# A two-block transformer kernel: 1/rms of the second block's norms applied behind the matmuls instead of to the rows

## The chip, the cores and the metric

One core of one Trainium2 chip. The metric is the device time of one execution in microseconds, median of several runs. Engines: TensorE (PE; its weight loads are PEld), VectorE (DVE), ScalarE (ACT), GpSimd (POOL), and SyncE (SP), which here only issues DMAs. Each engine runs its own instructions in order; semaphores order the engines against each other.

## What is computed

The input is 256 tokens of width 1024. A first block (three kinds of attention or recurrence, an output projection, a mixture of 16 experts) is followed by the second block, two layers of

```
h = h + 0.5 * swiglu(rmsnorm(h, g[0]), ...)      # feed-forward, 2816 wide
u = rmsnorm(h, g[1])
h = h + mixer(u)                                 # layer 0: hybrid attention, layer 1: sliding window
h = h + 0.5 * swiglu(rmsnorm(h, g[2]), ...)
...
def rmsnorm(x, g):
    return x * rsqrt(mean(x * x, -1) + EPS) * g
def swiglu(x, w1, w3, w2):
    return (silu(x @ w1) * (x @ w3)) @ w2
```

and a last rmsnorm. The factor rsqrt(...) is one number per token, so it can be applied to x, or to anything that is linear in x.

## The kernel before

**State.** x_res holds the 256 tokens as T = 2 blocks of 128 rows (tokens on partitions) by 1024 columns. All weights are streamed from HBM as "slots" of 128 x 3072 floats (1.5 MB), each in three pieces a, b, d of 512 KB. SP loads a piece into raw once the piece two slots earlier has been split. Matmuls run on rounded operands (fp32r), and every operand is split into a rounded part and its remainder: ACT writes w_hi (L546), DVE writes w_lo = raw - w_hi (L937). A product is three matmuls: hi by hi, hi by lo, lo by hi (L1537 to L1539; in feed-forward tiles L1718 to L1721 with hi and lo of x side by side, 512 columns).

**Feed-forward** (`feed_forward`, one version per engine): 22 tiles, one slot each. PE forms gate and up of 128 hidden columns (banks 4 to 7 of PSUM, alternating by tile), 16 steps over the 8 column blocks k of x; DVE sums the two halves of a bank (L1083), ACT takes silu (L670), DVE multiplies and splits h (L1107 to L1110); PE adds the down product of the tile before (banks 0 to 3). Behind the last tile DVE adds half of banks 0 to 3 into x_res (L1118), block 0 behind `y_tile`, block 1 behind `d_used`. The experts (`experts_by_group`) end in a scatter product and the same additions (L1177).

**Projections** (`proj`): a slot is three weight tiles of 128 columns. Results with tokens on partitions ("N", "W") are made for both blocks; those turned ("T") for all 256 tokens at once. ACT copies them out of PSUM (L569), or DVE adds them to x_res (L957). The hybrid layer has 8 slots, the sliding one 4, each output projection 3.

**A norm** (c = 0 to 11; 4, 5, 7, 8, 9, 11 belong to the second block's hidden state, 6 and 10 only turn the attention's output). In order: ACT squares both blocks with a running sum (L606, `ssq_ready`); POOL adds epsilon and takes the power -0.5 (L460, L462, `rstd_ready`); DVE scales block 0 (L970, `xs_ready`), ACT block 1 (L616, `xs1_ready`) into `scaled`; PE turns 16 squares of 128 x 128 into PSUM (L1543, `tr_ready` for each two column blocks); ACT rounds them times the gain into xT_hi (L628, `xt_hi`); DVE forms the remainder xT_lo (L982, `xt_lo`). PE starts the next stage as soon as the first two column blocks are there. While it waits it runs filler matmuls (`keep_busy`, L1550), 14 of them for one norm.

**Attention** works on units of one head pair and one token block: DVE adds the bias to the scores times a constant (L1003), and so on. The order of work on every engine is written out by hand.

Of the kernel before, what the change touches and what calls it, by code (L numbers as in the profile page):

```python
# [99 lines left out]
def block_program(nc, wstream, x_in, mem_in, pos_in, pos_cols_in, pcol_in, prow_in, smallw_in, const_in, table_in, bias_lookup_in,  # L100
                  bias_dram, out):
    ctx = ExitStack()
    with ctx:
# [24 lines left out]
        stat = sb("stat", [P, 256])  # L128
# [36 lines left out]
        def stats(n):  # L165
            o = taken[0]
            taken[0] += n
            assert taken[0] <= 256
            return stat[:, o:o + n]
# [18 lines left out]
        mqgain = stats(1)  # L188
        mixgain = stats(8)
# [77 lines left out]
        zb = at(16, 16, 2 * P)  # L267

# [27 lines left out]
        flat += [("T", v[:, j, :]) for v in (h_qaT, h_kaT, h_kbT) for j in range(4)]  # L296
# [3 lines left out]
        flat = [("T", s_qT[:, j, :]) for j in range(8)] + [("T", s_kT[:, j, :]) for j in range(2)] + [("N", s_v, 0)]  # L300
# [6 lines left out]
        def psum_places(n):  # L307
# [3 lines left out]
            n_first = [j for j, it in enumerate(tiles) if it[0] != "T"]  # L311
# [3 lines left out]
            for j, it in enumerate(tiles):  # L315
                if it[0] != "T":
# [52 lines left out]
        def g_of(i):  # L369
# [5 lines left out]
            dict(src=x_res, gain=g_of(0), norm=True), dict(src=x_res, gain=g_of(1), norm=True),  # L375
            dict(src=mixed, gain=onegain, norm=False), dict(src=x_res, gain=g_of(2), norm=True),
            dict(src=x_res, gain=g_of(3), norm=True), dict(src=x_res, gain=g_of(4), norm=True),
            dict(src=mixed, gain=onegain, norm=False), dict(src=x_res, gain=g_of(5), norm=True)]
# [4 lines left out]
        normed = [sum(n["norm"] for n in norms[:c]) for c in range(len(norms))]  # L383

        def turned(c, k):

            bank = k // 2 if c == 1 else 4 + k // 2
            return ps[:, bank, S * (k % 2):S * (k % 2) + S]

# [63 lines left out]
        def _(pool):  # L453
            def inverse_rms(i):

                pool.wait_ge(S_("ssq_ready"), i + 1)
                if i:
                    pool.wait_ge(S_("xs_ready"), i)
                    pool.wait_ge(S_("xs1_ready"), i)
                nc.gpsimd.tensor_scalar(meansq, ssq, RMS_EPS, None, ALU.add).then_inc(S_("meansq_ready"), 1)  # L460
                pool.wait_ge(S_("meansq_ready"), i + 1)
                nc.gpsimd.tensor_tensor(rstd, meansq, minus_half, ALU.pow).then_inc(S_("rstd_ready"), 1)  # L462

# [44 lines left out]
            pool.wait_ge(S_("y_added"), 2)  # L508
# [21 lines left out]
        def _(act):  # L530
# [24 lines left out]
            def evacuate_slot(n):  # L555

                act.wait_ge(S_("d_used"), n + 1)
                pair, n_first, places = psum_places(n)
                last = None
                groups = []  # L560
                for j, it, views in places:
                    if it[0] == "T":
                        groups.append((it[1], views[0]))
                    elif it[0] == "W":
                        groups += [(it[1][:, t, :], views[t][:, 0:8]) for t in range(T)]
                    else:
                        groups += [(it[1][:, t, it[2]:it[2] + P], views[t]) for t in range(T)]
                for dst, src in groups:
                    last = nc.scalar.activation(dst, src, ACT.Copy)  # L569
                last.then_inc(S_("evacuated"), 1)  # L570

# [15 lines left out]
            def norm(c, wait=None):  # L587
                norm_squares(c, wait)
# [3 lines left out]
            def norm_squares(c, wait=None):  # L592
                n = norms[c]
                if n["norm"]:
                    if c:
                        act.wait_ge(S_("xs_ready"), normed[c])
                    for t in range(T):

                        if c:
                            if wait[0] == "evacuated" and not t:  # L600
                                act.wait_ge(S_("half_added"), RESIDUAL_ENDS.index(wait[2]) + 1)
                            else:
                                act.wait_ge(S_(wait[0]), wait[1] + t if wait[0] == "y_added" else wait[1])
# [4 lines left out]
                    ins.then_inc(S_("ssq_ready"), 1)  # L608
# [12 lines left out]
            def norm_turned(c):  # L621
                n = norms[c]
                for q in range(4):
                    if c == 0 and q == 2:
                        split_hi(0, "d")
                    act.wait_ge(S_("tr_ready"), 4 * c + q + 1)
                    for k in (2 * q, 2 * q + 1):
# [1592 lines left out]
```

## Time and profile before

| | us |
|---|---|
| median of 3 runs (1635.41 to 1640.03) | 1635.64 |
| span of the profiled execution | 1634.7 |
| PE busy | 1552.5 (95%) |
| DVE busy | 1140.4 (70%) |
| ACT busy | 814.9 (50%) |
| mean granted TensorE clock | 0.984 of full speed |

The page says for each engine how much of the span it worked; the timeline gives single instructions with their start and length, and in brackets how long the engine had been idle before and who released it; windows give the same sums for chosen stretches. A busy PE may be running fillers. Times of the trace count from the first instruction.

### The profile page before, as it was taken

The page shows a single profiled execution, that of the slowest core. Times are in us where ns is not written, and L with a number is a line of the kernel's source. Part 1 is how long each engine was busy: PE and PEld are TensorE (multiplying, and loading weights), DVE is VectorE, ACT ScalarE, POOL GpSimd, SP SyncE. Part 2 cuts the span into 40 slices and gives each one's busy share as a digit, 9 for nine tenths or more (in the row PEclk, how much of TensorE's full clock was granted, in tenths as well). Part 3 has the DMA queues.
Part 4 walks back from the last instruction along what each step waited for, and adds up shares of the span by engine and source line. Part 5 has one row for each costly group of instructions (what it writes and reads, how often), then busy time and mean ns, then how long its engine had stood idle before and what let it go on. Part 6 is the DMA issues. An engine that isn't in the chain of part 4 may idle for free.

```text
span 1634.7 us, 27257 instructions
## 1 busy us (share of the span) xinstructions
PE 1552.5 (95%) x9282; PEld 1350.7 (83%) x9282; DVE 1140.4 (70%) x1741; ACT 814.9 (50%) x1309; POOL 45.2 (3%) x53
## 2 busy tenths in 40 slices
PE   7998798999999989999999999999999999999997
PEld 6887686888898958888898788888788878888886
DVE  5845864888798847777646567777777764677775
ACT  6423553777677744334544554443533355554442
POOL 1120000000000000000000200000000000000000
PEclk9999999999999999999999899999999999999999
DMA  7312231999799947555442355556455544255652
GB/s 260 116 62 81 78 113 37 323 348 344 257 345 344 354 169 225 190 185 187 137 155 78 106 185 188 191 192 193 155 187 184 188 136 154 78 166 186 189 191 77
DMA packets 82151, 299.70 MB, mean 183 GB/s; under 512 B 9279, under 2 KB 9407, under 8 KB 81953
## 3 DMA queue, kind: packets, MB, share of 16 engines
q1 hardware_dynamic: 79632, 289.97, 52.8%
q0 software_dynamic: 2160, 8.66, 1.7%
q8 instruction: 47, 0.77, 0.2%
q14 instruction: 24, 0.19, 0.0%
q10 hardware_dynamic: 288, 0.12, 0.0%
HBM read 297.59 MB, written 1.11 MB: 183 GB/s over the span
## 4 chain that ended last, share of the span: by engine, by line
PE 84%; DVE 9%; ACT 4%; issue 2%; POOL 1%; DMA 0%; DVEq 0%; SPq 0%; POOLq 0%; ACTq 0%
PE ps L1721 18%; PE ps L1537 15%; PE ps L1538 14%; PE ps L1539 14%; PE ps L1719 10%; PE ps L1718 3%; PE ps L1543 2%; DVE w_lo L937 2%; PE ps L1671 1%; PE ps L1814 1%; DVE xT L982 1%; PE ps L1738 1%; ACT w_hi L546 1%; PE ps L1643 1%; DVE stat L1005 1%
## 5 line engine op out<-in xcount | busy, mean ns | idle before, releaser
L937 DVE TENSOR_TENSOR w_lo<-raw,w_hi 128x1024 fp32r<-128x1024 f32 x549 | 653.6, 1221 | 216.3 <-ACT w_hi L546 214.8
L546 ACT ACTIVATE w_hi<-raw 128x1024 fp32r<-128x1024 f32 x549 | 549.2, 1055 | 339.8 <-PE ps L1539 307.3
L1721 PE MATMUL ps<-xT,w_hi 128*128 128x512 f32 x1232 | 439.6, 396 | 0.0
L1719 PE MATMUL ps<-xT,w_lo 128*128 128x256 f32 x1408 | 364.5, 279 | 0.0
L1719 PEld LDWEIGHTS ps<-xT,w_lo 128*128 128x128 f32 x1408 | 265.3, 188 | 16.1
L1721 PEld LDWEIGHTS ps<-xT,w_hi 128*128 128x128 f32 x1232 | 231.2, 188 | 47.1
L1537 PE MATMUL ps<-w_hi,xT 128*128 128x256 f32 (+2 forms) x848 | 261.6, 308 | 7.1 <-DVE w_lo L937 3.6
L1538 PE MATMUL ps<-w_lo,xT 128*128 128x256 f32 (+2 forms) x848 | 251.0, 296 | 0.0
L1539 PE MATMUL ps<-w_hi,xT 128*128 128x256 f32 (+2 forms) x848 | 250.7, 296 | 0.0
L1537 PE MATMUL ps<-w_hi,h_hi 128*128 128x512 f32 x480 | 188.4, 393 | 4.4 <-DVE h_lo L1143 4.4
L1538 PE MATMUL ps<-w_lo,h_hi 128*128 128x512 f32 x480 | 188.1, 392 | 0.0
L1539 PE MATMUL ps<-w_hi,h_lo 128*128 128x512 f32 x480 | 187.4, 391 | 0.0
L1537 PEld LDWEIGHTS ps<-w_hi,xT 128*128 128x128 f32 x848 | 160.8, 190 | 24.5 <-issue 21.3
L1538 PEld LDWEIGHTS ps<-w_lo,xT 128*128 128x128 f32 x848 | 161.3, 190 | 0.1
L1539 PEld LDWEIGHTS ps<-w_hi,xT 128*128 128x128 f32 x848 | 161.0, 190 | 0.0
L1083 DVE TENSOR_REDUCE arena<-ps 128x256 f32<-128x512 f32 x176 | 121.1, 688 | 38.2 <-PE ps L1721 38.2
L1543 PE MATMUL ps<-const,arena 128*128 128x128 f32 x416 | 76.7, 306 | 34.3 <-ACT arena L616 18.7
L1539 PEld LDWEIGHTS ps<-w_hi,h_lo 128*128 128x128 f32 x480 | 90.5, 189 | 19.7
L1537 PEld LDWEIGHTS ps<-w_hi,h_hi 128*128 128x128 f32 x480 | 90.5, 189 | 18.3 <-DVE h_lo L1143 4.7
L1538 PEld LDWEIGHTS ps<-w_lo,h_hi 128*128 128x128 f32 x480 | 90.5, 189 | 16.9
L1543 PEld LDWEIGHTS ps<-const,arena 128*128 128x128 f32 x416 | 53.8, 156 | 50.5 <-issue 20.2
L670 ACT ACTIVATE arena<-arena 128x256 f32<-128x256 f32 x88 | 36.8, 418 | 113.4 <-DVE arena L1083 113.4
(319 smaller groups left out, 1648.4 us busy)
## 6 DMA issues: line engine op xcount, KB each, us to landing
raw<-in_wstream SPq DMA_DIRECT2D x549, 512.0 KB, 4.9
arena<-bias_rows POOLq DMA_DIRECT2D x2, 2048.0 KB, 12.6
const<-in_const POOLq DMA_DIRECT2D x1, 1112.0 KB, 7.7
x_res<-in_x SPq DMA_DIRECT2D x2, 512.0 KB, 4.4
arena<-in_mem POOLq DMA_DIRECT2D x1, 1024.0 KB, 6.4
out<-arena SPq DMA_DIRECT2D x2, 512.0 KB, 2.7
smallw<-in_smallw POOLq DMA_DIRECT2D x1, 768.0 KB, 4.5
prow<-in_prow POOLq DMA_DIRECT2D x1, 512.0 KB, 5.2
```

The lines of the kernel that those rows point to most:

```text
L546: nc.scalar.activation(w_hi[:, slot, lo:hi], raw[:, slot, lo:hi], ACT.Copy).then_inc(S_(f"hi_{part_}"), 1)
L670: nc.scalar.activation(silu[:, f % 2, :], gate_sum[:, f % 2, :], ACT.Silu).then_inc(S_("silu_ready"), 1)
L937: tt(w_lo[:, slot, lo:hi], raw[:, slot, lo:hi], w_hi[:, slot, lo:hi].bitcast(F32), ALU.subtract).then_inc(S_(f"lo_{part_}"), 1)
L982: ins = stt(xT_lo[:, k, :], turned(c, k), n["gain"][:, k:k + 1], xT_hi[:, k, :].bitcast(F32), ALU.mult, ALU.subtract)
L1083: return nc.vector.tensor_reduce(dst[:, b, :], ps[:, bank, :].rearrange("p (a s) -> p s a", a=2), AX.X, ALU.add)
L1537: a = mm(out_, stat_[0], mov[0], start=start, stop=False)
L1538: b = mm(out_, stat_[0], mov[1], start=False, stop=False)
L1539: c = mm(out_, stat_[1], mov[0], start=False, stop=stop)
L1543: return nc.tensor.transpose(out_, in_, ident)
L1718: mm(bank, w_hi[:, s, c:c + P], both, start=True, stop=False)
L1719: low = mm(bank[:, 0:S], w_lo[:, s, c:c + P], xT_hi[:, k, :], start=False, stop=False)
L1721: last = mm(bank, w_hi[:, s, c:c + P], both, start=False, stop=k == KD - 1)
```

## The change

In norms 4, 5, 7, 8, 9 and 11 nothing is scaled in front of the turns any more: x_res itself is turned, rounded and split. 1/rms is applied later:
- feed-forward: DVE multiplies the gate sum by a row that holds 1/rms of each token (`rstd_row`), in every one of the 4 x 22 tiles; the up sum stays unscaled, and the final addition multiplies by 0.5/rms per token (`rstd_part`).
- projections: values and the other "N" results are scaled as ACT copies them (`scale=rstd`); keys (new kind "K", 9 hybrid tiles, 2 sliding ones) are written by DVE times `rstd_row` (`k_out`); queries stay unscaled, and the scores of kinds a and c are multiplied by 1/(8 rms) of the query token.
- `rstd_row` comes from two matmuls of PE (`rstd_rows`: 1/rms broadcast against the identity) and a copy by ACT (`rstd_row_out`). In a feed-forward they stand in the second tile, in a projection behind the first slot.

With it: the square of block 1 moves behind the rounding and the next slot's splits; turns stand in banks 0 to 3, 6 and 7, in groups (0), (1), (2), (3), (4, 5), (6, 7); behind an output projection the turns of column blocks 0 to 5 are done inside its last slot; the fillers go; piece d of the next slot is split by DVE behind the norm; the first tile or slot takes its steps by column block, gate and up together. `y_added` counts halves. The core of the diff:

```diff
@@ VectorE: norm, keys @@
-            def norm(c):
-                norm_scale(c)
-                norm_lo(c)
+            def norm(c, slot=None, after=None):
+                if not late[c]:
+                    norm_scale(c)
+                norm_lo(c, slot, after)
+
+            def k_out(n):
+                dve.wait_ge(S_("row_ready"), lates[5 if n < HOUT0 else 9] + 1)
+                dve.wait_ge(S_("d_used"), n + 1)
+                if all_k(n):
+                    dve.wait_ge(S_("evacuated"), evac_until(n - 1))
+                for dst, src in k_tiles(n):
+                    ins = tt(dst, src, rstd_row, ALU.mult)
+                ins.then_inc(S_("evacuated" if all_k(n) else "k_scaled"), 1)
...
@@ VectorE: end of norm_lo @@
+                if after == len(groups[c]):
+                    split_lo(slot, "d")
...
@@ ScalarE: norm @@
             def norm(c, wait=None):
+                if late[c]:
+                    norm_squares(c, wait, (0,))
+                    if c not in AFTER_FF:
+                        act.wait_ge(S_("d_used"), wait[2])
+                    norm_turned(c)
+                    return
...
@@ ScalarE: feed_forward tile, behind split_hi of a and b @@
+                    if c is not None and f == 0:
+                        norm_squares(c, wait, (1,))
+                        rstd_row_out(c)
...
@@ ScalarE: evacuate_slot @@
+                if n in k_slots:
+                    act.wait_ge(S_("k_scaled"), k_slots.index(n) + 1)
...
@@ VectorE: feed_forward tile @@
-                    summed(gate_sum, 4 + 2 * b).then_inc(S_("gate_summed" if f0 else "moe_gate_summed"), 1)
+                    def gate_scaled():
+                        dve.wait_ge(S_("gate_raw"), plus(at_f + f + 1, i, per))
+                        tt(gate_sum[:, b, :], gate_sum[:, b, :], rstd_row, ALU.mult).then_inc(S_("gate_summed"), 1)
+
+                    summed(gate_sum, 4 + 2 * b).then_inc(S_("moe_gate_summed" if gated else "gate_raw"), 1)
+                    if f and not gated:
+                        gate_scaled()
                     if n + 1 < N_SLOTS:
                         split_lo(n + 1, "b", i, per)
                     dve.wait_ge(S_("b_used"), plus(n + 1, i, per))
                     summed(up_sum, 5 + 2 * b).then_inc(S_("up_summed" if f0 else "moe_up_summed"), 1)
+                    if not f and not gated:
+                        dve.wait_ge(S_("row_ready"), lates[c] + 1)
+                        gate_scaled()
...
-                    if n + 1 < N_SLOTS:
+                    if f < tiles - 1:
                         split_lo(n + 1, "d", i, per)
...
-                        ins = stt(x_res[:, t, 512 * half:512 * half + 512], ps[:, 2 * t + half, :],
-                                  1.0 if gated else 0.5, x_res[:, t, 512 * half:512 * half + 512], ALU.mult, ALU.add)
-                    ins.then_inc(S_("y_added"), 1)
+                        stt(x_res[:, t, 512 * half:512 * half + 512], ps[:, 2 * t + half, :],
+                            1.0 if gated else rstd_part[:, t:t + 1], x_res[:, t, 512 * half:512 * half + 512], ALU.mult,
+                            ALU.add).then_inc(S_("y_added"), 1)
...
@@ TensorE @@
+            def late_norm(c):
+                y = 4 * AFTER_FF[c]
+                pe.wait_ge(S_("y_added"), y + 2)
+                for k in (0, 1, 4, 5, 6, 7):
+                    turn(c, k, 0)
+                pe.wait_ge(S_("y_added"), y + 3)
+                turn_last(c, 0)
+                turn_last(c, 1)
+                turn_both(c, 2)
+                pe.wait_ge(S_("y_added"), y + 4)
+                turn_both(c, 3)
+                turn_last(c, 4, 5)
+                turn_last(c, 6, 7)
+
+            def late_norm_open(c, n):
+                pe.wait_ge(S_("evacuated"), evac_until(n - 1))
+                for k in range(4):
+                    turn_both(c, k)
+                turn_both(c, 4, 5)
+
+            def late_norm_close(c, n):
+                pe.wait_ge(S_("half_added"), RESIDUAL_ENDS.index(n + 1) + 1)
+                turn(c, 6, 0)
+                turn(c, 7, 0)
+                pe.wait_ge(S_("evacuated"), evac_until(n))
+                turn_last(c, 6, 7)
+
+            def rstd_rows(c):
+                pe.wait_ge(S_("rstd_ready"), normed[c] + 1)
+                for t in range(T):
+                    ins = mm(ps[:, 0, P * t:P * t + P], rstd[:, t:t + 1].broadcast_to([P, P]), ident, start=True, stop=True)
+                ins.then_inc(S_("row_psum"), 1)
...
@@ TensorE: feed_forward tile @@
+                        if f == 1 and not g and k == KD // 2 and call is not None:
+                            rstd_rows(call)
...
@@ TensorE: down product @@
+                    if not f and call is not None:
+                        pe.wait_ge(S_("row_ready"), lates[call] + 1)
...
-            norm(7, added=("evacuated", evac_until(FFB0 - 1)))
+            late_norm_close(7, FFB0 - 1)
             feed_forward(*ffs[2], 7)
-            norm(8, added=("y_added", 6))
+            late_norm(8)
```

## Rows read from the trace of the kernel before

**Rows 1.** The page, part 1: busy us of the engines, share, instructions.

```profile
PE 1552.5 (95%) x9282; PEld 1350.7 (83%) x9282; DVE 1140.4 (70%) x1741; ACT 814.9 (50%) x1309; POOL 45.2 (3%) x53
```

**Rows 2.** Windows at six norms: length; busy PE, PEld, DVE, ACT, POOL; clock; DMA; GB/s.

```profile
604.63:612.69 8.06, 6.54 (x33) 4.13 (x31) 3.06 (x6) 4.20 (x9) 2.48 (x3) 1.00 0.19 65
795.84:804.22 8.38, 6.12 (x31) 3.96 (x30) 3.96 (x8) 5.33 (x11) 0.94 (x2) 1.00 0.00 0
953.70:960.52 6.82, 5.74 (x33) 4.06 (x31) 2.20 (x5) 4.66 (x11) 0.94 (x2) 1.00 0.41 147
1143.66:1152.02 8.36, 6.12 (x31) 3.97 (x30) 3.96 (x8) 5.33 (x11) 0.93 (x2) 1.00 0.01 4
1335.16:1343.52 8.36, 6.12 (x32) 3.97 (x30) 3.97 (x8) 5.33 (x11) 0.93 (x2) 1.00 0.01 4
1435.16:1441.96 6.80, 5.73 (x33) 4.05 (x31) 2.20 (x5) 4.66 (x11) 0.93 (x2) 1.00 0.39 145
```

**Rows 3.** Timeline at norm 8: start, us, engine, line, operation, tiles, [idle before <-releaser].

```profile
1142.07 0.39 PE L1539 MATMUL ps<-w_hi,h_lo 128*128 128x512 f32 x1
1142.23 1.23 DVE L937 TENSOR_TENSOR w_lo<-raw,w_hi 128x1024 fp32r<-128x1024 f32 x1 [1.87 <-ACT w_hi L546]
...
1143.38 2.48 DVE L1118 SCALAR_TENSOR_TENSOR x_res<-ps,x_res 128x512 f32<-128x512 f32 x4
...
1143.43 0.39 PE L1539 MATMUL ps<-w_hi,h_lo 128*128 128x512 f32 x1
...
1144.75 1.06 ACT L606 ACTIVATE arena<-x_res 128x1024 f32<-128x1024 f32 x1 [2.55 <-DVE x_res L1118]
...
1145.90 3.26 PE L1550 MATMUL ps<-xT 128*128 128x512 f32 x10 [1.18 <-DVE x_res L1118]
...
1147.42 0.71 POOL L462 TENSOR_TENSOR stat<-stat 128x2 f32<-128x2 f32 x1
...
1149.46 1.94 PE L1543 MATMUL ps<-const,arena 128*128 128x128 f32 x16 [0.30 <-ACT arena L616]
1150.12 3.03 ACT L628 ACTIVATE xT<-ps,pcol 128x256 fp32r<-128x256 f32 x8 [0.81 <-PE ps L1543]
1151.00 3.23 DVE L982 SCALAR_TENSOR_TENSOR xT<-ps,pcol,xT 128x256 fp32r<-128x256 f32 x8 [2.08 <-ACT xT L628]
...
1152.02 0.47 PE L1718 MATMUL ps<-xT,w_hi 128*128 128x512 f32 x1 [0.62 <-DVE xT L982]
...
1155.08 0.40 PE L1718 MATMUL ps<-xT,w_hi 128*128 128x512 f32 x1
```

**Rows 4.** Timeline at norm 7: the last matmul of the projection and the addition behind it.

```profile
953.58 0.28 PE L1539 MATMUL ps<-w_hi,xT 128*128 128x256 f32 x1
...
953.90 0.42 DVE L957 TENSOR_TENSOR x_res<-ps,x_res 128x256 f32<-128x256 f32 x1 [0.99 <-PE ps L1539]
```

**Rows 5.** Timeline at norm 4: the additions of block 1 behind the experts.

```profile
605.23 1.29 DVE L1177 TENSOR_TENSOR x_res<-ps,x_res 128x512 f32<-128x512 f32 x2 [5.58 <-PE ps L1814]
```

**Rows 6.** Twenty steady tiles of a feed-forward (windows), and a 256-wide DVE multiply (groups).

```profile
1160.30:1324.50 164.20, 164.20 (x870) 140.70 (x869) 119.00 (x160) 64.72 (x78) 0.00 (x0) 1.00 0.60 192
...
L1107 DVE TENSOR_TENSOR h_hi<-arena 128x256 fp32r<-128x256 f32 x88 | 37.5, 426 | 15.7 <-DVE arena L1083 15.1
```

**Rows 7.** Hybrid projections: timeline of ACT, of DVE, then the window behind them.

```profile
864.15 1.06 ACT L569 ACTIVATE arena<-ps 128x256 f32<-128x256 f32 x5 [4.36 <-PE ps L1539]
...
872.48 1.13 ACT L569 ACTIVATE arena<-ps 128x128 f32<-128x128 f32 x6 [3.40 <-PE ps L1539]
...
867.39 3.50 DVE L937 TENSOR_TENSOR w_lo<-raw,w_hi 128x1024 fp32r<-128x1024 f32 x3
...
871.00:883.00 12.00, 12.00 (x69) 11.20 (x67) 0.00 (x0) 6.25 (x16) 0.00 (x0) 1.00 0.36 116
```

**Rows 8.** Windows in front of norm 10: no matmul issued, then the clock.

```profile
1408.00:1409.00 1.00, 0.00 (x1) 0.00 (x0) 0.89 (x4) 0.00 (x0) 0.00 (x0) 1.00 0.00 0
1409.50:1412.50 3.00, 3.00 (x16) 3.00 (x16) 1.24 (x3) 2.09 (x6) 0.00 (x0) 0.50 0.00 0
```

More of the change, by code:

```diff
@@ L310, in psum_places @@
             tiles = projections[n]
-            n_first = [j for j, it in enumerate(tiles) if it[0] != "T"]
+            n_first = [j for j, it in enumerate(tiles) if it[0] not in "TK"]
             at_n = len(n_first) * P
@@ L383, in block_program, with k_tiles, all_k @@
         normed = [sum(n["norm"] for n in norms[:c]) for c in range(len(norms))]
+        late = ["late" in n for n in norms]
+        lates = [sum(late[:c]) for c in range(len(norms))]
+        early_scaled = [sum(n["norm"] and "late" not in n for n in norms[:c]) for c in range(len(norms) + 1)]
+        groups = [((0,), (1,), (2,), (3,), (4, 5), (6, 7)) if late[c] else ((0, 1), (2, 3), (4, 5), (6, 7))
+                  for c in range(len(norms))]
+        group_base = [sum(len(g) for g in groups[:c]) for c in range(len(norms))]
+        LATE_BANK = (0, 1, 2, 3, 6, 6, 7, 7)
+        AFTER_OUT = {FFB0: 7, FFD0: 11}
+        AFTER_FF = {4: 0, 5: 1, 8: 2, 9: 3}
         def turned(c, k):
+            if late[c]:
+                col = S * (k % 2) if k >= 4 else 0
+                return ps[:, LATE_BANK[k], col:col + S]
             bank = k // 2 if c == 1 else 4 + k // 2
             return ps[:, bank, S * (k % 2):S * (k % 2) + S]
+        def k_tiles(n):
+            pair, n_first, places = psum_places(n)
+            return [(it[1], views[0]) for j, it, views in places if it[0] == "K"]
+        def all_k(n):
+            return n in projections and len(k_tiles(n)) == len(projections[n])
+        k_slots = [n for n in projections if n in range(HYB0, HOUT0) or n in range(SWA0, SOUT0)]
+        k_slots = [n for n in sorted(k_slots) if k_tiles(n) and not all_k(n)]
         ffs = [(MOE0, MOE_TILES, 0), (FFA0, FF_TILES, MOE_TILES), (FFB0, FF_TILES, MOE_TILES + FF_TILES),
@@ L659, in attention, with feed_forward @@
                         exp_unit(i)
-            def feed_forward(n0, tiles, f0):
+            def feed_forward(n0, tiles, f0, c=None, wait=None):
                 def tile(f, i=None, per=0):
@@ L1576, in transposed @@
             def transposed(c, k):
-                if c is not None and k % 2 == 0:
-                    pe.wait_ge(S_("xt_lo"), 4 * c + k // 2 + 1)
+                if c is not None:
+                    for g, ks in enumerate(groups[c]):
+                        if ks[0] == k:
+                            pe.wait_ge(S_("xt_lo"), group_base[c] + g + 1)
             def proj(n, c=None):
@@ L1706, in tile @@
                         pe.wait_ge(S_("h_ready"), plus(f0 + f - 1, i, per))
-                    for g in range(2):
-                        if not g or not by_k:
-                            for part_ in "ab" if by_k else "ab"[g]:
+                    both_first = by_k or not f
+                    steps = [(g, k) for g in range(2) for k in range(KD)]
+                    if not f:
+                        steps.sort(key=lambda s: s[1])
+                    for g, k in steps:
+                        if not k and not (g and both_first):
+                            for part_ in "ab" if both_first else "ab"[g]:
                                 pe.wait_ge(S_(f"hi_{part_}"), plus(n + 1, i, per))
@@ L2014, in _ @@
                 feed_forward(*ffs[0], None)
-            norm(4, added=("y_added", 2))
+            late_norm(4)
             feed_forward(*ffs[1], 4)
-            norm(5, added=("y_added", 4))
+            late_norm(5)
             proj(HYB0, 5)
+            rstd_rows(5)
             proj(HYB0 + 1)
@@ L2066, in _ @@
                 proj(n, 10 if n == SOUT0 else None)
-            norm(11, added=("evacuated", evac_until(FFD0 - 1)))
+            late_norm_close(11, FFD0 - 1)
             feed_forward(*ffs[4], 11)
```

227 lines of the change are left out of this document (143 added, 84 removed).

## Prediction

> **What bounds the kernel now.** I read the page's engine line first: TensorE (PE) is busy 95% of the span, VectorE (DVE) 70%, ScalarE (ACT) 50% [rows 1]. So time can come only out of places where PE has no useful matmul to run. Next I cut the trace at the six norms that the change touches (norms 4, 5, 7, 8, 9, 11; 7 and 11 stand behind an output projection, the others behind an expert or feed-forward stage). Each window of [rows 2] runs from the issue of the first thing behind the last useful matmul to the issue of the first matmul of the next stage: 8.06, 8.38, 6.82, 8.36, 8.36 and 6.80 us, 46.8 us in all. PE looks busy in them (5.7 to 6.5 us), but that is filler matmuls and the 16 turns. The timeline of norm 8 [rows 3] shows what the window is made of, one thing behind the other: DVE still splits the last piece of the next slot (1142.23 to 1143.46) though the first half of PE's sums was there earlier; four additions into x_res; two Squares on ACT; the pow on POOL, ended 1148.13; the scaling of the rows; 16 turns from 1149.46; ACT's rounding from 1150.12; DVE's remainder from 1151.00; first matmul 1152.02. Everything between the additions and the turns is there only for 1/rms.
>
> **The change, part by part.** All sums are against the profiled execution, whose span is 1634.7 us; the median of the runs is 1635.64, 0.9 above it, and I keep that distance.
>
> *Norm behind a feed-forward (norms 5, 8, 9; clock times are norm 8's).* DVE's split of piece d moves behind the norm, so the additions of block 0 wait only for PE's matmul of 1142.07, which ends 1142.46. An addition starts 0.04 behind the end of its matmul (953.58 + 0.28, then 953.90) [rows 4], so 1142.50. From the first addition to the first Square it took 1144.75 - 1143.38 = 1.37 [rows 3], so Square of block 0 runs 1143.87 to about 1145.0. The matmul of 1143.43 ends 1143.82, so block 1 is added from 1143.86, one half in 0.62 (2.48 / 4). Its first half releases the turn of column block 0 at 1144.5; from turn to ACT took 0.66 for four turns, for one about 0.4, so ACT is ready for it at 1145.0, just as Square ends. One rounding 0.43, one remainder 0.44 and 0.14 to PE (the steps of [rows 3], halved because the first group now holds one column block, not two): first matmul at 1146.1, a gap of 2.44. Saved: 8.38 - 2.44 = 5.94, and 5.92 twice.
>
> *Norm behind the experts (norm 4).* Block 0's Square is over long before; block 1's additions start at 605.23 [rows 5]. 0.65 for one half, 0.4, 0.43, 0.44, 0.14 give 607.35 against 612.69: 5.34 saved.
>
> *Norm behind a projection (norms 7, 11).* Twelve turns move into the last slot's matmuls: they now lengthen it, at (1.94 - 0.27) / 15 = 0.11 each by 1.33. After the last matmul (953.58 + 0.28 for norm 7) [rows 4] ACT's rounding can start at once, it waits for the slot's end only because it overwrites xT; DVE's addition (0.42) runs beside it. 0.04 + 0.43 + 0.45 + 0.14 behind the end: gap 1.25 counted from the window's start. Saved 6.82 - 1.33 - 1.25 = 4.24, and 4.22.
>
> Together 31.6 us.
>
> *The first tile.* It now takes gate and up by column block, 5.5 / 8 = 0.69 of matmuls each against 0.40 for one remainder (3.23 / 8), so nothing starves; before, the first half tile took 1155.08 - 1152.02 = 3.06 [rows 3], where the pace of the steady tiles is (8.21 - 12 x 0.227) / 2 = 2.75 (8.21 from [rows 6], 0.227 from the six matmuls between 1142.07 and 1143.43). That gives back 0.3 at four norms and 0.15 at the two in front of a projection: +1.5. The two matmuls that spread 1/rms into a row are new on PE: no row shows this form; between 0.11 (a turn at full clock) and twice that (at half), I take 0.12 each plus their semaphore, 0.25 per norm: -1.5. At norm 9 the moved split of piece d follows the remainders (ends about 1341.5) and PE wants it at about 1341.2: -0.3.
>
> *What moves off the chain but stays work.* The Square of block 1 now stands on ACT behind the rounding and two splits of the next slot. For norm 8: rounding 1145.0 to 1147.9, splits until 1150.0; first Square's start to pow's end was 3.38 with two Squares, so 2.3 with one: 1/rms at 1152.3. PE asks for it in the middle of the second tile's gate, 1146.1 + 5.5 + 1.4 = 1153.0. Slack 0.7, so cost zero; the cover is the first tile. Queued behind this wait on PE is the rest of that tile; ACT waits too (row copy, then silu). DVE sums the first gate until 1152.5, splits a piece until 1153.6, sums up until 1154.3, multiplies by the row (there at 1154.1) until 1154.7; silu, three short DVE operations: h at about 1156.4. The first down product asks for it at 1146.1 + 2 x 5.5 + 0.25 = 1157.4. If the chain were late, each us late costs a us, up to about 2 per norm.
>
> *The added multiply of the gate sum.* 88 tiles, each one DVE multiply of 128x256: 0.43 [rows 6]. In the steady state DVE works 119.0 of 164.2 us (20 tiles) and PE 164.2 of 164.2 [rows 6], so 5.95 of 8.21 per tile becomes 6.4. Free while that holds. The chain gate sum, multiply, silu, h is longer by 0.45, and h is wanted a tile later (in the last tile behind the 2.7 us of the down product before it). Constants in the final addition and the scores become per-partition columns; the remainder, which reads such a column, takes 0.40 per 256 elements, no more than the plain multiply, so zero.
>
> *Keys.* Nine key tiles of the hybrid stage and two of the sliding one are now written by DVE (0.43 each, about 3.9 us) instead of ACT. DVE has nothing at all from 871 to 883 while PE is full [rows 7], which hides it. The tight place is slot 5 of the hybrid stage: ACT emptied it at 864.15, now it waits for DVE's multiply, which stands behind the index scores, where DVE's splits of slot 7 began (867.39, later by one multiply of three tiles less what ACT's lighter queue brings forward): about 868.2. The splits of slot 7 slip with it by 3 to 4 us, the first piece to about 871.4, wanted at 872.4, where slot 6 ends (ACT empties it at 872.48). Slack 1.0; the load behind it lands later too. I put 0.1 there and 0.2 on the last sliding slot, where ACT waits for one DVE multiply in front of the attention: -0.3. Bounds 0 and 3.
>
> Sum: 31.6 + 1.5 - 1.5 - 0.3 - 0.3 = **31.0 us**. Span 1603.7, median **1604.6**.
>
> *The fillers.* 14 wide filler matmuls per norm go. In the trace PE had nothing to run from 1408 to 1409, behind a run of short matmuls, and right behind that the granted clock was 0.50, 1.2 GHz, for three us [rows 8]. In the new gaps the idle stretches are shorter (turns stand between them, about 0.3 each; about 0.8 behind a projection) and dense matmuls stand in front of them; in the windows of [rows 2], with idle stretches of up to 1.18 (the filler of 1145.90) [rows 3], the clock stayed at 1.00, 2.4 GHz. So I count no loss.
>
> The Trainium skill, "TensorE: Matmul & The Clock Gate", section "What's actually happening", says that the throttled clock is the default and that activity releases it. That speaks against taking fillers out. The trace agrees that the clock can fall at a boundary; whether the new boundaries are quiet enough no row says. By the rule taken strictly the time would be the first rival's 1614.8.
>
> **The rivals.**
> *The clock falls at the six boundaries.* For: the stretch of [rows 8]. Against: less idle time than in today's windows. Three to four us of matmuls at half clock cost 1.5 to 2, I take 1.7: six of them 10.2, time 1614.8.
> *PE waits for 1/rms in the second tile.* For: slack of only 0.7, with ACT's loads and splits in front. Against: nothing on ACT there waits for data today. Late by 1.5 at each norm: 9 us, time 1613.6.
> *It does only half of what it says.* Another wait, the weights' splits or PSUM banks that turns and sums now share, ends last in the gaps: 2.5 us lost at each norm: 15, time 1619.6.
> *Slower: DVE becomes the bound of the steady tiles.* The gate multiply sits before silu in the loop. It decides once DVE needs over 8.21 us per tile. Each of 88 tiles would then be longer by up to 0.43, 38 us on top of 1604.6: 1642.4. Against: 1.8 us of room per tile.
>
> **How the numbers follow.** Forecast 0.74, clock 0.12, 1/rms 0.07, half 0.04, slower 0.03. The likeliest case alone spans 1600 to 1609 (bounds of keys, row matmuls, and the low-clock stretches in the attention, which may fall elsewhere when everything before them moves: one more or less is 1.7). For 8 in 10 the upper end reaches to the first two rivals: 1599 to 1615. 0.3% of this kernel is 4.9 us, about what can be told from no change. Faster 0.96, within 0.01, slower 0.03.
>
> **What the profile would show.** Gaps between the last useful matmul and the next of about 2.4 us (2.7 at norm 4; behind projections 1.25, with 12 turns inside the last slot). ACT's rounding starting as block 0's Square ends. No PE idle in front of the two row matmuls. Steady windows of 164.2 us for 20 tiles as before, with DVE at about 128. Clock 1.00 in the first tile behind each norm. It is wrong if a steady tile is longer than 8.21, if PE idles over 0.5 in the second tile, or if the hybrid stage up to its attention is longer than before by over 1 us.

## The result: 0.5% faster, 28 us slower than predicted

| | before | after |
|---|---|---|
| median | 1639.74 us (20 runs) | 1632.31 us (20 runs, 1617.62 to 1643.87) |
| span of the profiled execution | 1634.7 | 1640.6 |
| mean granted clock, profiled | 0.984 | 0.957 |

Time after / before is 0.9947, 95% interval 0.9925 to 0.9968; this ratio leaves out slow executions, those over 1.5% above the fastest of their kernel. 1604.6 was predicted, with 1599 to 1615 as the range. The forecast was counted down from 1635.64, the median of three runs; over 20 runs the kernel before takes 1639.74. So 4.1 of the 27.7 us by which the forecast missed lie in its starting point, and 23.6 in the change: 31.0 us were to be saved, the medians differ by 7.4. The spread of the changed kernel is wide, and it goes with the granted clock: its 20 executions have mean clocks from 0.956 (1641.6 us) to 0.976 (1617.6 us).

The page of after, its parts 1 and 2 (busy us; the clock in 40 slices of the span, tenths of full speed), answers [rows 1]:

```profile
PE 1570.0 (96%) x9222; PEld 1370.7 (84%) x9222; DVE 1175.8 (72%) x1834; ACT 808.9 (49%) x1298; POOL 50.5 (3%) x59
...
PEclk9998999999999999999998599999999997799999
```

The same line of before:

```profile
PEclk9999999999999999999999899999999999999999
```

PE executes fewer matmuls (9222 for 9282) but is busy 17.5 us longer. The two dips of after, slices 22 to 23 and 34 to 35, are the two attention stages of the second block.

The six gaps and the twelve early turns of norms 7 and 11 as windows (columns as in [rows 2]: length; busy PE, PEld, DVE, ACT, POOL; clock; DMA), then 20 steady tiles, which answer [rows 6]:

```profile
611.24:613.69 2.45, 2.29 (x17) 1.67 (x16) 1.92 (x4) 1.14 (x4) 0.00 (x0) 1.00 0.03 10
797.08:799.66 2.58, 2.35 (x17) 1.72 (x17) 2.26 (x5) 2.17 (x6) 0.00 (x0) 1.00 0.01 3
963.53:964.87 1.34, 0.82 (x6) 0.38 (x5) 1.05 (x3) 1.14 (x4) 0.00 (x0) 1.00 0.90 284
1148.28:1150.87 2.59, 2.35 (x18) 1.73 (x17) 2.26 (x5) 2.18 (x6) 0.00 (x0) 1.00 0.00 0
1334.32:1336.90 2.58, 2.34 (x17) 1.72 (x17) 2.26 (x5) 2.17 (x6) 0.00 (x0) 1.00 0.01 3
1446.20:1447.54 1.34, 0.82 (x7) 0.38 (x5) 1.06 (x3) 1.14 (x4) 0.00 (x0) 1.00 0.84 333
959.36:960.59 1.23, 1.23 (x15) 1.23 (x13) 1.23 (x2) 0.00 (x0) 0.00 (x0) 1.00 0.70 77
...
1161.00:1325.20 164.20, 164.20 (x871) 140.72 (x870) 127.44 (x182) 68.06 (x81) 0.00 (x0) 1.00 0.60 196
```

The gaps were to be 2.7 (norm 4), 2.44 (norms 5, 8, 9) and 1.25 behind 1.33 of early turns. They are 2.45, 2.58, and 1.34 behind 1.23, all at full clock. Against [rows 2] they save 5.61 + 5.80 + 4.25 + 5.77 + 5.78 + 4.23 = 31.4 us; 31.6 was forecast. What took it back is in the windows of after's attention stages, and two of before beside them:

```profile
890.00:934.00 44.00, 43.93 (x179) 33.84 (x179) 21.87 (x45) 18.46 (x66) 10.66 (x8) 0.50 0.11 36
1378.00:1415.00 37.00, 37.00 (x165) 30.34 (x165) 17.53 (x39) 18.65 (x70) 0.00 (x0) 0.50 0.00 1
```

```profile
894.00:904.00 10.00, 9.79 (x42) 7.24 (x40) 6.36 (x16) 4.86 (x19) 1.96 (x2) 0.50 0.01 2
1383.00:1408.00 25.00, 24.35 (x190) 19.71 (x189) 17.47 (x42) 19.79 (x76) 0.00 (x0) 1.00 0.01 2
```

After works most of its attention at 1.2 GHz: 165 matmuls of the sliding stage take 37 us where before 190 took 25. Cutting both traces at the same points gives the whole sum (positive: after is longer):

| part | us |
|---|---|
| before norm 4, code the change doesn't touch (37.5 us at 0.50 in after, 23.9 in before, 34.1 in a second trace of before) | +6.6 |
| six gaps | -31.4 |
| feed-forwards +0.24, +0.27, +0.31, +0.18, end +0.12 | +1.1 |
| hybrid projections up to the first scores (78.19 to 79.20) | +1.0 |
| hybrid output projection +0.73 (still at 0.50 where it starts), sliding one -0.06 | +0.7 |
| sliding projections up to the first scores (35.32 to 36.71) | +1.4 |
| hybrid attention, first scores to norm 6 (45.18 to 56.59) | +11.4 |
| sliding attention, first scores to norm 10 (30.45 to 46.23) | +15.8 |
| norm 10 (before 3.27, at low clock; after 2.59, at full) | -0.7 |
| sum, and the difference of the spans | +5.9 |

### The profile page after: what moved, and what is told of

The parts are those of the page before. It is cut to its first block, busy times and chain, and to the rows that moved or that the text cites. A ratio compares the mean times of both kernels' runs of the same rounds, so it can differ in the third digit from the quotient of the medians.

```text
span 1640.6 us, 27255 instructions
## 1 busy us (share of the span) xinstructions
PE 1570.0 (96%) x9222; PEld 1370.7 (84%) x9222; DVE 1175.8 (72%) x1834; ACT 808.9 (49%) x1298; POOL 50.5 (3%) x59
## 4 chain that ended last, share of the span: by engine, by line
PE 88%; DVE 8%; ACT 2%; issue 1%; DMA 0%; DVEq 0%; POOL 0%; SPq 0%; POOLq 0%; ACTq 0%
PE ps L1888 17%; PE ps L1634 15%; PE ps L1635 14%; PE ps L1636 14%; PE ps L1886 10%; PE ps L1640 3%; PE ps L1885 3%; PE ps L1831 2%; PE ps L1803 2%; DVE w_lo L1001 2%; PE ps L1981 1%; PE ps L1905 1%; DVE xT L1059 1%; ACT w_hi L580 1%; PE ps L2063 1%
## 5 line engine op out<-in xcount | busy, mean ns | idle before, releaser
L1640 PE MATMUL ps<-const,arena 128*128 128x128 f32 x320 | 71.9, 342 | 29.7 <-ACT arena L670 16.1
L1640 PEld LDWEIGHTS ps<-const,arena 128*128 128x128 f32 x320 | 47.0, 175 | 47.4 <-issue 25.7
```

The source lines that it names most:

```text
L1640: return nc.tensor.transpose(out_, in_, ident)
```

## The experiments

Three questions: is the low clock in the attention the change's doing or chance, what tips it, and what is the change worth without it? The table gives medians, mean clock of the profiled execution, the two attention stages in its trace (first scores to the turns of norm 6 and of norm 10), and the low-clock stretch that begins around the scores of the hybrid stage's sixth unit, where PE has waited for DVE to finish the fourth (the expectations call it the fourth unit). "None" means none there: several traces have a second stretch of 3.4 or 6.8 us at the end of the hybrid stage or behind it, e3 among them.

| kernel | median us | clock | hybrid | sliding | low stretch, sixth hybrid unit |
|---|---|---|---|---|---|
| before | 1638 to 1640 | 0.984 | 45.2 | 30.5 | 10.2 |
| c1 before again | 1638.3 | 0.983 | 44.2 | 30.5 | 10.2 |
| after | 1632.3 | 0.957 | 56.6 | 46.2 | 51.2 |
| c2 after again | 1633.4 | 0.963 | 48.5 | 48.3 | 23.9 |
| c3 after, fillers in sliding | 1627.9 | 0.981 | 48.3 | 35.3 | 23.9 |
| c4 before, same fillers | 1644.7 | 0.978 | 45.2 | 35.6 | 10.2 |
| d1 after, fillers only at its start | 1615.5 | 0.974 | 48.6 | 31.6 | 23.9 |
| d2 after, sliding keys as before | 1631.5 | 0.955 | 56.6 | 47.7 | 51.2 |
| d3 after, fillers in the gaps | 1634.0 | 0.970 | 48.6 | 46.3 | 23.9 |
| d4 c3 and two per hybrid unit | 1615.7 | 0.987 | 43.4 | 35.3 | none |
| e1 before, late sliding start | 1657.2 | 0.968 | 45.2 | 48.1 | 10.2 |
| e2 after, best fillers | 1608.8 | 0.990 | 43.4 | 31.6 | none |
| e3 before, same fillers | 1638.2 | 0.984 | 42.9 | 31.3 | none |
| e4 after, constant in hybrid scores | 1626.5 | 0.967 | 44.4 | 48.3 | 10.2 |
| f1 before, column in hybrid scores | 1640.2 | 0.988 | 44.6 | 30.4 | 10.2 |
| f2 e4 again | 1620.8 (2 runs) | 0.968 | 48.1 | 48.2 | 23.9 |

**Both kernels again (c1, c2).**

> The kernel before, unchanged, for its granted clock in many executions. In the profiled execution of the changed kernel, time lost to low clock has a price of its own: both attention stages of the second block ran at 0.50 nearly throughout (45.2 to 56.6 us and 30.5 to 46.2 us, first scores to the turns of norms 6 and 10). Theory A (the change moves these stages into the low clock): here the clock is 0.98 to 0.985 in most executions, and the two stages are near 45 and 30.5 us in the profile. Rival B (the low clock falls on the attention by chance in either kernel, and the profiled execution of before was a lucky one): clocks spread over 0.96 to 0.985, and a second profile shows one of the two stages over 10 us longer.

> The changed kernel, unchanged, for a second trace. Theory A: the two attention stages are again at 0.50 for most of their length (about 56 and 46 us), whatever the first block does. Rival B: at least one of them is at full clock (45 or 30 us) here. The gaps at the six norms stay at 2.5 us (1.3 behind the projections) in either case.

Before: ratio 0.9985 (0.9959 to 1.0011), all 12 executions at clock 0.974 to 0.988. After: 0.9897 (0.9811 to 0.9983). Of 86 executions of the kernel before with a recorded clock, 5 took 1655 us or more, at 0.960 to 0.970; of 24 of the changed kernel, 22 were at 0.972 or below. So the low clock comes with the change (theory A), though not with it alone: before falls into it now and then.

**Fillers in the sliding attention (c3, c4).**

```diff
-                if u < ATT4[0]:
-                    keep_busy(ps[:, 2 * (u % 2), :], 1)
+                keep_busy(ps[:, 2 * (u % 2), :], 1)
...
-                    if i == u0 + 1 and u0 == ATT2[0]:
+                    if i == u0 + 1 and u0 in (ATT2[0], ATT4[0]):
                         keep_busy(ps[:, 7 - u0 // QUAD % 2, :], 10)
...
+            keep_busy(ps[:, 0, :], 6)
             pe.wait_ge(S_("evacuated"), evac_until(SOUT0 - 1))
             attention(*ATT4)
```

> The changed kernel with filler matmuls in the sliding attention as the hybrid one has them: six in front of it, ten behind its second unit, one (0.21 us) ahead of each unit's scores. At full clock they cost at most 32 x 0.21 = 6.8 us less what PE waits there (about 4): up to 3 us. Theory A with few columns per us as what keeps the clock low: the sliding attention runs at full clock, 46.2 us become 31 to 34, time 1632.3 - 12 to 15 = about 1619. Rival C (the clock's fall comes from something other than the attention's own matmuls): the stage stays at 0.50 and gets longer by the fillers at half clock, 32 x 0.43 = up to 13 us, time 1635 to 1645.

> The kernel before with the same fillers in the sliding attention. Its stage ran at full clock in the profile (30.5 us), so fillers can't win there: theory A expects 0 to 3 us more than before (1636 to 1643). Rival B (before falls low there in many executions too): up to 5 us less in the median.

In the trace of c3 the sliding stage is at full clock, 35.3 us. Its median moved less than expected (1627.9, not 1619): four of nine executions took 1611.9 to 1620.5, at clocks from 0.977, the others 1627.9 to 1633.5 at 0.966 to 0.973, and of these there is no trace. In before the fillers lengthen the stage by 5.1 us in the trace (35.6 for 30.5), where 0 to 3 was expected; over all executions the ratio is 1.0025 (0.9996 to 1.0053), which leaves no cost just possible. One filler per unit lies on the path.

**Where the fall starts (d1, d2).** d1 keeps c3's last two edits and drops the first. d2 makes the two sliding keys kind "T" again, copied by ACT, and gives their scores a constant (the sliding keys and queries lack 1/rms).

```diff
-        flat = [("T", s_qT[:, j, :]) for j in range(8)] + [("K", s_kT[:, j, :]) for j in range(2)] + [("N", s_v, 0)]
+        flat = [("T", s_qT[:, j, :]) for j in range(8)] + [("T", s_kT[:, j, :]) for j in range(2)] + [("N", s_v, 0)]
```

> The changed kernel with fillers only where the sliding attention starts: six behind the projections, ten behind the second unit, none ahead of the other units. Theory A1 (what makes the clock fall is the quiet stretch at the stage's start, 1372.3 to 1377.9 in the changed kernel, where PE works 2.9 of 5.8 us; once low it stays low): the stage runs at full clock, about 31 us, the clock of the run is 0.975 or more, time about 1615 to 1620, and as good as with fillers ahead of each unit (1627.9 in the median, 1617.6 in the profiled execution). Rival A2 (the units' own matmuls have too few columns, fillers ahead of each are needed): the stage is at 0.50 for most of its length, time about 1632.

> The changed kernel with the sliding keys as before: ACT copies them unscaled, DVE multiplies nothing, and the scores get a constant instead of a column (so the sliding keys and queries lack 1/rms, and the scores are scaled down to stay in range). Theory A3 (the keys' way over DVE makes the quiet stretch at the start 0.5 us longer, and that tips the clock): PE waits 0.8 us for the first scores instead of 1.34, the stage is at full clock in most executions as in the kernel before, clock 0.97 to 0.98, time about 1618. Rival A4 (the delay is not what tips it): stage at 0.50 for 45 us, time about 1632.

d1: 1615.5 (4 runs, 1609.0 to 1619.7), ratio 0.9842 (0.9818 to 0.9866), sliding stage 31.6. Fillers at the start alone do it, with the units' own matmuls unchanged: A2 falls, and A1 fits. The start of the stage on PE in before, after and d1 (timelines: start, us, engine, line, tiles, [idle before]):

```profile
1378.84 0.93 PE L1643 MATMUL ps<-arena 64*128 64x128 f32 x8 [0.81 <-ACT arena L569]
1380.37 0.49 PE L1643 MATMUL ps<-arena 64*128 64x128 f32 x4 [0.61 <-DVE stat L1005]
1381.29 0.44 PE L1543 MATMUL ps<-const,arena 128*128 128x128 f32 x2 [0.42 <-ACT arena L637]
...
1383.31 0.56 PE L1671 MATMUL ps<-arena 128*128 128x64 f32 x4
```

```profile
1373.61 0.93 PE L1803 MATMUL ps<-arena 64*128 64x128 f32 x8 [1.34 <-issue]
1375.30 0.49 PE L1803 MATMUL ps<-arena 64*128 64x128 f32 x4 [0.76 <-DVE stat L1085]
1376.21 0.44 PE L1640 MATMUL ps<-const,arena 128*128 128x128 f32 x2 [0.42 <-ACT arena L691]
...
1378.71 0.95 PE L1831 MATMUL ps<-arena 128*128 128x64 f32 x4
```

```profile
1362.11 1.55 PE L1647 MATMUL ps<-xT 128*128 128x512 f32 x6
1363.59 0.93 PE L1803 MATMUL ps<-arena 64*128 64x128 f32 x8
1364.44 2.57 PE L1647 MATMUL ps<-xT 128*128 128x512 f32 x10
```

PE waits 0.81 + 0.61 + 0.42 in front of its first three groups in before, 1.34 + 0.76 + 0.42 in after: 0.68 longer. The last row of the first two shows the fall: the same four matmuls take 0.56 in before and 0.95 in after. Why it is longer stands on ACT and DVE (before in the first two views, after in the third):

```profile
1378.06 0.72 ACT L569 ACTIVATE arena<-ps 128x256 f32<-128x256 f32 x3 [4.46 <-PE ps L1539]
```

```profile
1379.44 0.42 DVE L1003 SCALAR_TENSOR_TENSOR arena<-ps,arena 128x256 f32<-128x256 f32 x1 [4.20 <-issue]
```

```profile
1372.88 0.63 ACT L611 ACTIVATE arena<-ps,stat 128x128 f32<-128x128 f32 x2 [4.73 <-PE ps L1636]
...
1372.37 0.42 DVE L1038 TENSOR_TENSOR arena<-ps,arena 128x256 f32<-128x256 f32 x1 [2.58 <-PE ps L1636]
1374.30 0.48 DVE L1083 SCALAR_TENSOR_TENSOR arena<-ps,stat,arena 128x256 f32<-128x256 f32 x1 [1.51 <-PE ps L1803]
```

DVE's key stands in front of ACT's two copies (0.5), and the score operation takes 0.48 instead of 0.42. d2 takes the key away, but the first two waits are still 1.04 and 0.71 where A3 had counted on 0.8 for the first, and the stage is still low in its trace (47.7), with executions at 0.955 and 0.960 beside ones at 0.971 and 0.980. A3 is not borne out as written: the key alone doesn't decide. No run brings the wait of the changed kernel back to 0.81.

**The gaps (d3).** Fillers around the turns of norms 4, 5, 8 and 9, with the identity as weights; behind an output projection (norms 7 and 11) there are only two, behind the last turns:

```diff
+            def keep_warm(n):
+                for _ in range(n):
+                    mm(ps[:, 4, 0:S], ident, const[:, 0:S], start=True, stop=True)
...
+                keep_warm(2)
                 pe.wait_ge(S_("y_added"), y + 2)
                 for k in (0, 1, 4, 5, 6, 7):
                     turn(c, k, 0)
+                keep_warm(1)
...
                 turn_last(c, 6, 7)
+                keep_warm(2)
```

> The changed kernel with filler matmuls back in the six gaps: two of 0.43 us (128 wide weights, 256 columns, full precision) in front of the turns, one in the middle, two behind them. They cost about 0.6 to 1 us per gap, 4 to 6 us in all. Rival B2 (the change pays for the fillers it took out: the chip's clock remembers the boundaries): the attention stages run at full clock more often, clock 0.97 or more, time 1620 to 1628. Theory A (the attention's clock is decided by what stands at the attention): nothing changes there, clock 0.955 to 0.97, time 1636 to 1639.

1634.0, sliding stage 46.3, hybrid 48.6. Both stages are still low with the gaps filled, and the time is outside B2's 1620 to 1628: B2 is not borne out. The clock of its ten executions, 0.963 to 0.973, is somewhat above after's, so a small effect isn't excluded.

**The delay put into before (e1).**

```diff
+                if n == SOUT0 - 1:
+                    groups[-1:-1] = [(scaled[:, 0, P * e:P * e + P], groups[-1][1]) for e in range(3)]
                 for dst, src in groups:
                     last = nc.scalar.activation(dst, src, ACT.Copy)
```

> The kernel before with one edit: in the last sliding projection slot ACT makes three idle copies of 128x128 (about 0.2 us each) ahead of its last one, so that PE waits about 1.4 us for the first scores instead of 0.81, as it does in the changed kernel (1.34). Nothing else differs: norms, fillers and scores are the old ones. Theory A1 (a quiet stretch at the start that is 0.6 us longer is enough to tip the clock for the whole stage): the sliding attention falls to 0.50 in most executions, 30.5 us become 46, clock about 0.965 instead of 0.982, median 1650 to 1656. Rival A6 (the tipping needs something else that the change brings): the stage stays at full clock as in the kernel before, median 1640, one execution in ten long.

All seven executions took 1652.6 to 1659.0; ratio 1.0104 (1.0073 to 1.0134). Its timeline and a window of the stage:

```profile
1381.16 0.93 PE L1645 MATMUL ps<-arena 64*128 64x128 f32 x8 [1.32 <-ACT arena L571]
1382.69 0.49 PE L1645 MATMUL ps<-arena 64*128 64x128 f32 x4 [0.61 <-DVE stat L1007]
```

```profile
1386.00:1424.00 38.00, 38.00 (x172) 31.34 (x171) 17.72 (x41) 19.07 (x72) 0.00 (x0) 0.50 0.00 1
```

Half a microsecond more of waiting (1.32 for 0.81) at the start of a 30 us stage costs 17.6 us (48.1 for 30.5), with none of the change in the kernel. That such a wait is enough is shown by this; that it is the whole of what tips the changed kernel is likely by d1 and e1, not shown.

**Hybrid stage (d4, e4, f1, f2).** d4 is c3 with two fillers ahead of each hybrid unit. e4 and f2 put a constant into after's hybrid scores of kind a (their queries lack 1/rms), f1 a column into before's (a wrong factor). The first two lines are e4 and f2, the others f1:

```diff
-                    scale = rstd_part[:, un["t"]:un["t"] + 1] if un["kind"] in "ac" else HD ** -0.5
+                    scale = rstd_part[:, un["t"]:un["t"] + 1] if un["kind"] == "c" else HD ** -0.5 * (1e-3 if un["kind"] == "a" else 1)
...
-                    ins = stt(dst, src, HD ** -0.5, z, ALU.mult, ALU.add)
+                    scale = rstd[:, un["t"]:un["t"] + 1] if un["kind"] == "a" else HD ** -0.5
+                    ins = stt(dst, src, scale, z, ALU.mult, ALU.add)
```

> The kernel with fillers in the sliding attention (one per unit, six and ten at its start), and two instead of one ahead of each unit's scores in the hybrid attention, where its profile still showed 24 us in one piece at 0.50. At full clock 16 more fillers cost up to 3.4 us, less what PE waits there. Theory A: the hybrid stage falls to low clock for 0 to 10 us instead of 24, 5 to 9 us gained, 0 to 3 paid: median about 1620 against 1627.9. Rival C2 (the fall is at the fourth unit whatever the fillers): stage longer by 3 to 6 us, median 1631.

> The changed kernel with a constant instead of the column in the scores of the hybrid attention's kind a (their queries lack 1/rms, and the constant is smaller to stay in range). DVE's operation on 256 columns should take 0.42 us again instead of 0.48. Theory A7 (the 0.06 to 0.12 us that each unit's path gained there make the hybrid stage's low stretch longer): it is 10 to 17 us as in the kernel before instead of 24 to 51, median about 1627. Rival A8 (something else lengthens it): 24 us or more again, median 1632.

> The kernel before with a column (1/rms of the query's token, a wrong factor here) instead of the constant 1/8 in the scores of the hybrid attention's kind a; nothing else differs. Theory A7 (the slower operation on the scores, 0.48 instead of 0.42 us for 256 columns, makes the hybrid stage's low stretch longer): the first low stretch of the stage is 24 to 51 us instead of 10.2, as in the changed kernel, and the median is 4 to 10 us above the kernel before, 1643 to 1649. Rival A8 (the change's effect there comes from elsewhere): 10.2 us again, median 1639.

> The changed kernel with the constant in the hybrid scores of kind a once more, for a second trace. Theory A7: its hybrid stage is low for 10.2 us in one piece again. Rival A8: 24 or 51 us, and the first trace was chance.

d4: hybrid stage 43.4 with no stretch at 0.50, median 1615.7 (4 runs), ratio 0.9858 (0.9842 to 0.9875): A holds. e4's trace fitted A7 (10.2 us low), f1 (10.2 where 24 or more was expected) and f2 (23.9) speak against it. These are single traces, and f1's is the fastest of its ten executions: four of the ten took 1643.5 us or more, of 13 executions of before measured beside them none. So A7 isn't settled. The traces do have one thing in common: the filler ahead of the sixth unit's scores. In before, after and e4:

```profile
893.27 0.50 PE L1550 MATMUL ps<-xT 128*128 128x512 f32 x1 [0.79 <-DVE stat L1005]
```

```profile
890.07 0.79 PE L1647 MATMUL ps<-xT 128*128 128x512 f32 x1 [0.85 <-DVE stat L1085]
```

```profile
887.30 0.72 PE L1647 MATMUL ps<-xT 128*128 128x512 f32 x1 [0.79 <-DVE stat L1085]
```

Where it ran at full clock (0.50: before, c1, c4, e1, f1) the stretch lasted 10.2 us every time. Where the clock fell before or during it (0.57 to 0.80: after, c2, c3, d1, d2, d3, e4, f2) it lasted 10.2 once, 23.9 five times and 51.2 twice. In the first five the clock falls 0.42 to 0.88 us behind the start of this filler. In the other eight it falls between 0.39 before and 0.28 behind it, and the two stretches of 51.2 us are the two earliest falls (0.38 and 0.39 before). So the clock falls there in both kernels, some tenths of a microsecond earlier against the work in the changed one, and the length goes with that. Whether it is the cause isn't shown: the first five are all versions of the kernel before, the other eight of the changed one. Which edit moves the fall is open, and the nearest rival wasn't tried: the hybrid stage too starts later behind its projections (by 0.54 us), as the sliding one does.

**The change at full clock (e2, e3).** Both kernels with c3's last two edits and

```diff
-                    keep_busy(ps[:, 2 * (u % 2), :], 1)
+                    keep_busy(ps[:, 2 * (u % 2), :], 1 if u < ATT2[0] else 2)
```

behind the old `if u < ATT4[0]`, so that, other than the expectation says, the sliding units have none.

> The changed kernel with the fillers that paid: six in front of the sliding attention, ten behind its second unit, two ahead of each unit's scores in both attentions of the second block. Each of the two places alone gave about 1615.6. Theory A (both stages at full clock): clock 0.985, median 1610 to 1616. Rival (two fillers per unit in the sliding attention, 16 x 0.21 = 3.4 us more, lie on the path for nothing): 1617 to 1620.

> The kernel before with the same fillers, so that both kernels run their attentions at full clock and the difference to the changed kernel with fillers is the change alone. By the stages of the two profiles (gaps 31.4 us shorter, the rest 3.5 us longer) the changed kernel should be 28 us faster: this one at 1638 to 1644 where that one is at 1610 to 1616. Rival (the change saves less than the gaps show, because the low clock hides a cost elsewhere): difference under 23 us.

e2: 1608.75 (5 runs, 1608.0 to 1612.0), ratio 0.9817 (0.9777 to 0.9857). e3: 1638.2, ratio 0.999 (0.9969 to 1.0011). Their difference is 29.5 us in the medians, 30.6 in the spans (1606.4 and 1637.0). Part of it is still clock: e3's trace has 6.8 us at 0.50 behind its hybrid stage and 3.4 at norm 10, e2's has neither. At one and the same clock, 0.987, e2 took 1609.5 and e3 1636.4 to 1638.4: 27 to 29 us apart. e2 is the fastest kernel here, 23.6 us ahead of after. Its two stages in windows:

```profile
868.00:918.00 50.00, 44.94 (x282) 32.43 (x281) 32.40 (x73) 26.14 (x88) 10.70 (x9) 1.00 0.12 38
1350.00:1380.00 30.00, 29.86 (x222) 23.55 (x221) 20.57 (x44) 21.87 (x80) 0.00 (x0) 1.00 0.13 49
```

## Why the prediction missed

*The gaps: right.* 31.4 for 31.6. Norm 8 went as the steps say (timeline of after, to be read beside [rows 3]):

```profile
1147.18 2.73 DVE L1210 SCALAR_TENSOR_TENSOR x_res<-ps,stat,x_res 128x512 f32<-128x512 f32 x4 [2.21 <-PE ps L1636]
...
1148.05 0.39 PE L1636 MATMUL ps<-w_hi,h_lo 128*128 128x512 f32 x1
...
1148.65 2.19 PE L1640 MATMUL ps<-const,x_res 128*128 128x128 f32 x16 [0.21 <-DVE x_res L1210]
1148.69 1.06 ACT L659 ACTIVATE arena<-x_res 128x1024 f32<-128x1024 f32 x1 [1.87 <-DVE x_res L1210]
...
1149.74 3.01 ACT L682 ACTIVATE xT<-ps,pcol 128x256 fp32r<-128x256 f32 x8
...
1150.87 0.47 PE L1885 MATMUL ps<-xT,w_hi 128*128 128x512 f32 x1
```

ACT's rounding starts as Square ends (its accumulator is read out until 1149.83), as said, 0.12 later than in the steps. The four additions, which now read a column, take 2.73 where 2.48 was counted. Norm 4 took 2.45 for 2.7.

*First tile and row matmuls: 1.2 off in the feed-forwards.* The two matmuls that spread 1/rms, full precision, take 0.36 (1157.98 to the next matmul at 1158.34), not 0.25, and the first tile by column block gives back 0.05 to 0.18, not 0.3: each feed-forward is 0.2 to 0.3 longer than before where 0.05 shorter was expected. The power and the row matmuls behind norm 8:

```profile
1156.15 0.71 POOL L492 TENSOR_TENSOR stat<-stat 128x2 f32<-128x2 f32 x1
...
1157.75 0.65 PEld L1700 LDWEIGHTS ps<-const,stat 128*128 128x128 f32 x4
1157.98 0.61 PE L1700 MATMUL ps<-const,stat 128*128 128x128 f32 x4
```

*1/rms in time: right.* The power ends at 1156.86, PE begins to load it as weights at 1157.75 and doesn't wait: 0.9 us of slack, 0.7 was said. The rival "PE waits for 1/rms" is out.

*Gate multiply: right.* 20 tiles in 164.20, DVE 127.4 for 128. The slower rival, DVE as the bound, is out.

*Keys: under-sized.* Norm 9's late piece cost PE 0.31 (0.3 said). In front of the sliding attention I put 0.2; it was 0.53. In front of the hybrid one I had nothing: ACT's six copies with a column take 1.66 instead of 1.13, and the first scores come 0.54 later behind the projections. The copies of after, beside those of 872.48 in [rows 7]:

```profile
876.71 1.66 ACT L611 ACTIVATE arena<-ps,stat 128x128 f32<-128x128 f32 x6 [0.83 <-PE ps L1636]
```

That columns in place of constants cost zero was wrong for both engines: 0.28 for 0.19 per copy on ACT, which the prediction didn't price at all, and 0.48 for 0.42 on DVE. So the hybrid projections lost 1.0 us where 0.2 was forecast, just at the prediction's own sign of being wrong ("by over 1 us"), and the sliding ones 1.4 where 0.6 was. With the feed-forwards and the end (1.1) the stages cost 3.5 us, the gaps save 31.4, and the change is worth 28 us by the stages and 27 to 29.5 by e2 and e3, not 31. That alone would have left the time inside the range.

*The clock of the attention: the step that failed.* The sum had no term for the two attention stages, and the range gave their low-clock stretches "one more or less is 1.7", with 3 us as the length of a stretch, from [rows 8]. In the two traces of the changed kernel the stretch at the sixth hybrid unit is 51 and 24 us long and the one in the sliding stage 38 and 48, and in the profiled execution the two stages lost 11.4 and 15.8 us: 27.2 where nothing was counted and 1.7 allowed. "So I count no loss" was argued for the six boundaries only, and there it holds: clock 1.00 in every gap. The clock rival looked at the same boundaries, priced a fall there at 1.7 us each, and is out too. What the steps didn't ask is what the edits do to a stage that stands near a fall already. The sliding keys' 0.2 us and the columns' zero were taken as costs in time alone; the wait that they lengthen, from 0.81 to 1.34 us, is of the size that tipped the stage in e1. [rows 8] showed the fall behind the sliding attention; the view of its start, 1378 to 1383 in before, with the same kind of waits, I didn't read.

The Trainium skill, "TensorE: Matmul & The Clock Gate", section "What's actually happening", says that the gate is set by how busy PE has recently been. The windows of after speak against reading that off the profile's busy column: PE is busy 43.93 of 44.00 us and 37.00 of 37.00, and the clock is 0.50 all along, while before keeps 1.00 with 24.35 of 25.00.

## What to carry over

Half a microsecond added in front of a stage of short matmuls cost 17.6 us in e1, over half of what the whole change saves: after an edit upstream, read the granted clock of every such stage, also where its code is the same, and compare several executions by their clock. Put fillers where PE waits at the stage's start (16 of 0.21 us: 16.8 us gained here); ahead of each unit they cost what they take, 3.7 us in the sliding stage. To learn what an edit is worth, give both kernels the same fillers and compare executions of the same clock.

## What the runs showed that was not expected

- The same work ran at either clock: the sliding stage at 0.50 for 37 us with PE busy throughout, and at 1.00 for its whole length when 16 fillers stood at its start. Once low, it stayed so for 38 to 51 us in seven traces. The hybrid stage came back to 1.00 in its midst in most traces; what ends a stretch isn't shown.
- 0.51 us more idle time (0.81 to 1.32) turned 5 executions in 86 with a clock of 0.970 or less into 7 in 7 with 0.973 or less.
- A per-partition column as scale costs ACT 0.09 us per 128x128 copy (six in 1.66 for 1.13) and DVE 0.06 per 256 columns (0.48 for 0.42).
- The fall at the hybrid stage's sixth unit came in every trace with one filler per unit, and its length took three values only: 10.2, 23.9 and 51.2 us.
